# Second attention: scores four steps ahead of the transposes, and three smaller reorderings

## The reference

```python
# first block, mixer: cb, cc, ch are three projections of the normalized x
y_conv = cb * causal_dwconv3(cc * ch, conv_w)
y_conv = group_rms_norm(y_conv, conv_norm_g, CONV_GROUPS)
h = h + concatenate([y_conv, y_ret]) @ w_out
# second block, 8 heads of 64 of each kind, causal, 512 x 512
y_fox = softmax(q_f @ k_f.T / 8 + F[t] - F[s]) @ v_f          # F: cumulative log forget gate
sel   = top_k(sum_h w_i[t, h] * relu(q_i @ k_i.T / 8), 128)    # keys that each query may see
y_dsa = softmax(q_d @ k_d.T / 8 + bias, over sel) @ v_d
merged = sigmoid(gate_fox) * (y_fox @ w_branch_fox) + sigmoid(gate_dsa) * (y_dsa @ w_branch_dsa)
x = x + gate1 * (merged @ w_out)
```

## Time and profile before

| | us |
|---|---|
| median of three runs | 1446.51 |
| profiled execution | 1447.23 |
| its span | 1445.4 |
| PE busy | 1378.2 (95%) |
| DVE busy | 807.1 (56%) |
| POOL busy | 570.1 (39%) |
| ACT busy | 515.1 (36%) |

### The profile page before, as it was taken

The page is one execution under the profiler, slowest core; times in us unless marked ns, Lnnn a source line. Parts: engine busy times, 40 slices in busy tenths (PEclk is TensorE's granted clock), DMA queues, the critical chain, the costliest instruction groups (busy, mean ns, idle before and its releaser), DMA issues.

```text
span 1445.4 us, 18266 instructions
## 1 busy us (share of the span) xinstructions
PE 1378.2 (95%) x6154; PEld 1099.1 (76%) x6158; DVE 807.1 (56%) x1096; ACT 515.1 (36%) x771; POOL 570.1 (39%) x230
## 2 busy tenths in 40 slices
PE   7899999999999999999888889999989999999997
PEld 5677777888788888876665566788868888888886
DVE  6555567484765847868877676311235534253353
ACT  4333224332323323234345455423344323142243
POOL 3334334454462634424212122344433645445341
PEclk9999999999999999989999999999999999999998
DMA  7643234365574646522312222233332423324221
GB/s 199 130 88 91 70 102 132 104 180 153 153 204 142 187 129 179 135 73 74 88 44 72 60 74 73 73 102 102 94 95 73 130 74 115 88 86 117 73 88 58
DMA packets 238985, 155.46 MB, mean 108 GB/s; under 512 B 7860, under 2 KB 229424, under 8 KB 238808
## 3 DMA queue, kind: packets, MB, share of 16 engines
q1 hardware_dynamic: 238472, 153.56, 37.9%
q10 hardware_dynamic: 464, 1.27, 0.3%
HBM read 150.08 MB, written 4.73 MB: 107 GB/s over the span
## 4 chain that ended last, share of the span: by engine, by line
PE 42%; DVE 11%; issue 1%; ACT 0%; another core or an unknown queue 0%; DVEq 0%; ACTq 0%
PE ps L504 35%; PE ps L870 3%; DVE work L1744 2%; DVE top L1742 2%; PE ps L783 1%; PE ps L771 1%; DVE prob L1784 1%; DVE probt_even L1799 1%; DVE work L1762 1%; DVE prob L1792 1%; PE ps L757 1%; DVE xres L1695 0%; PE ps L758 0%; DVE q_dn L1811 0%; DVE work L1759 0%
## 5 line engine op out<-in xcount | busy, mean ns | idle before, releaser
L467 POOL TENSOR_TENSOR w_lo<-raw,w_hi 128x1024 fp32r<-128x1024 f32 x222 | 566.2, 2558 | 843.4 <-ACT w_hi L940 838.6
L504 PE MATMUL ps<-u_hi,w_hi 128*128 128x512 f32 x1016 | 411.2, 405 | 18.7 <-DVEq L1814 6.9
L504 PE MATMUL ps<-u_hi,w_lo 128*128 128x512 f32 x1016 | 399.8, 394 | 0.0
L504 PE MATMUL ps<-u_lo,w_hi 128*128 128x512 f32 x1016 | 399.7, 393 | 0.0
L940 ACT ACTIVATE w_hi<-raw 128x1024 fp32r<-128x1024 f32 x221 | 231.7, 1053 | 209.8 <-PE ps L504 106.0
L504 PEld LDWEIGHTS ps<-u_hi,w_hi 128*128 128x128 f32 x1016 | 193.7, 191 | 66.6 <-issue 16.1
L504 PE MATMUL ps<-y_hi,w_hi 128*128 128x512 f32 x576 | 225.9, 392 | 1.5 <-POOL w_lo L467 1.4
L504 PE MATMUL ps<-y_hi,w_lo 128*128 128x512 f32 x576 | 224.9, 390 | 0.0
L504 PEld LDWEIGHTS ps<-u_hi,w_lo 128*128 128x128 f32 x1016 | 193.2, 190 | 41.7
L504 PE MATMUL ps<-y_lo,w_hi 128*128 128x512 f32 x576 | 224.8, 390 | 0.0
L504 PEld LDWEIGHTS ps<-u_lo,w_hi 128*128 128x128 f32 x1016 | 193.7, 191 | 40.5 <-issue 2.2
(11 more groups left out here) (228 smaller groups left out, 1396.7 us busy)
## 6 DMA issues: line engine op xcount, KB each, us to landing
raw<-w_in SPq DMA_DIRECT2D x69, 512.0 KB, 3.8
raw<-w_mlp SPq DMA_DIRECT2D x64, 512.0 KB, 4.0
adaw<-w_ada SPq DMA_DIRECT2D x32, 768.0 KB, 4.6
raw<-w_up SPq DMA_DIRECT2D x32, 512.0 KB, 6.2
raw<-w_down SPq DMA_DIRECT2D x32, 512.0 KB, 6.7
raw<-w_out SPq DMA_DIRECT2D x16, 512.0 KB, 3.8
bias_rows<-fbrow SPq DMA_DIRECT2D x4, 640.0 KB
xtok<-x SPq DMA_DIRECT2D x4, 512.0 KB, 6.1
```

Of the source, the lines that this page charges most:

```text
L467: pool.tensor_tensor(w_lo[:, s, :], raw[:, s, :], w_hi[:, s, :], ALU.subtract).then_inc(lo_ready[s], 1)
L504: last = pe.matmul(ps[0:cols, bank, :], w[:, s, c], r[:, k, :], start=(k == ks[0] and w is w_hi and r is r_hi), stop=(k == ks[-1] and w is ...
```

## The change

PE now makes the scores of tile-step n + 4 right behind the transposes of n, across the pairs' borders, with one part of a projection (two chunks, 6 matmuls) behind each; `prob` has four buffers. The projections run further ahead, and in the last pairs the gate units of two merge chunks are made. The merge then makes `branch(m - 1)` behind the units of chunk m, with banks in turn. DVE's and ACT's orders follow, the rounds are spread 13, 2, 1, 1, 1, 1, 1 ahead of the pairs and five in each of pairs 0 to 3, the last even copy goes to ACT (`turned_last`), and two reciprocals become one. In the convolution the third unit is begun ahead of `conv_sum`, and in the first output projection the casts stand two steps earlier.

```diff
+LOOK = 4
...
+    bra_order = [(0, 0), (1, 0)]
+    for m in range(KC):
+        bra_order += [(0, m + 1), (1, m + 1), (2, m)] if m + 1 < KC else [(2, m)]
...
+        prob_evens = sb("prob_evens", [P, 2, KEYROW], where=odd)
...
+        gates = sb("gates", [P, 4, T], where=keys_done)
...
-        prob = sb("prob", [P, 2, T], where=two)
+        prob_odds = sb("prob_odds", [P, 2, T], where=two)
...
+        def prob(n):
+            return (prob_evens, prob_odds)[n // 2 % 2][:, n % 2, 0:(n // 2 + 1) * P]
...
-            with pe.Fori(1, NQ) as j:
+            for j, cut in ((1, 5), (2, 3), (3, 0)):
                 unit(st_conv, 0, j, u_hi, u_lo)
                 unit(st_conv, 1, j, u_hi, u_lo)
+                if cut:
+                    unit(st_conv, 2, j, u_hi, u_lo, part=(0, cut), closes=False)
                 conv_sum(j - 1)
-                unit(st_conv, 2, j, u_hi, u_lo)
+                unit(st_conv, 2, j, u_hi, u_lo, part=(cut, KC), opens=(cut == 0))
...
-                if n >= 2:
-                    pe.wait_ge(sem("att_logit"), 8 * p + n - 1)
+                wait(pe, sem("att_logit"), 8 * p + n - 1)
...
-            def att(pieces, p, dsa):
-
-                def piece():
-                    pieces.pop(0)()
-                piece()
-                s_step(p, 0, dsa)
-                s_step(p, 1, dsa)
-                if p > 0:
-                    pv(p - 1)
-                piece()
-                for a in range(3):
-                    t_step(p, 2 * a)
-                    s_step(p, 2 * a + 2, dsa)
-                    t_step(p, 2 * a + 1)
-                    s_step(p, 2 * a + 3, dsa)
-                    piece()
-                t_step(p, 6)
-                t_step(p, 7)
-                piece()
-
-            def thirds(st, g):
-                def one(s, k0, k1):
-                    return lambda: unit(st, s, g, u_hi, u_lo, part=(k0, k1), opens=(k0 == 0), closes=(k1 == KC))
-                return [one(s, k0, k1) for s in range(2) for k0, k1 in ((0, 3), (3, 6), (6, KC))]
+            def pairs(st, s, i):
+                def one(k0):
+                    return lambda: unit(st, s, i, u_hi, u_lo, part=(k0, k0 + 2), opens=(k0 == 0), closes=(k0 + 2 == KC))
+                return [one(k0) for k0 in range(0, KC, 2)]
...
-            for s in range(2):
-                unit(st_att, s, 0, u_hi, u_lo)
-            for g in range(1, 2 * NQ):
-                att(thirds(st_att, g), g - 1, g > NQ)
-
+            pieces = [f for g in range(2 * NQ) for s in range(2) for f in pairs(st_att, s, g)]
+            pieces += [f for m in range(2) for s in range(2) for f in pairs(st_bra, s, m)]
+            for _ in range(KC + LOOK - 2):
+                pieces.pop(0)()
+            for n in range(LOOK):
+                pieces.pop(0)()
+                s_step(0, n)
+            for p in range(2 * NQ):
+                for n in range(8):
+                    if n == 0 and p > 0:
+                        pv(p - 1)
+                    t_step(p, n)
+                    coming = 8 * p + n + LOOK
+                    if coming < 16 * NQ:
+                        s_step(coming // 8, coming % 8)
+                    pieces.pop(0)()
 
             def branch(m):
                 pe.wait_ge(lo_ready[2], st_bra.turn(2, m) + 1)
-                wait(pe, bank_free[2], st_bra.turn(2, m))
-                for b, k0 in ((2, 0), (SA, NQ)):
+                wait(pe, bank_free[2], st_bra.turn(2, m) - 1)
+                for b, k0 in ((2 + m % 2, 0), (SA + m % 2, NQ)):
                     for k in range(k0, k0 + NQ):
                         pe.wait_ge(sem("att_y"), k + 1)
                         c = slice(k * P, (k + 1) * P)
@@ -872,13 +880,16 @@
                                              stop=(k == k0 + NQ - 1 and w is w_lo))
                 last.then_inc(used[2], 1)
 
-            att(thirds(st_bra, 0), 2 * NQ - 1, True)
+            pieces.pop(0)()
             pv(2 * NQ - 1)
+            for f in pieces:
+                f()
             branch(0)
-            with pe.Fori(1, KC) as m:
+            for m in range(2, KC):
                 unit(st_bra, 0, m, u_hi, u_lo)
                 unit(st_bra, 1, m, u_hi, u_lo)
-                branch(m)
+                branch(m - 1)
+            branch(KC - 1)
...
                 ahead(st_conv, 1, j)
+                ahead(st_conv, 2, j)
                 conv_root(j - 1)
-                ahead(st_conv, 2, j)
...
-                    if i > 0 or s >= AHEAD:
-                        ahead(st_out, s, i)
+                    n = i * 4 + s + AHEAD
+                    if n < KC:
+                        ahead(st_out, n % 4, n // 4)
...
+            def exps(p, n):
+                act.wait_ge(sem("att_logit"), 8 * p + n + 1)
+                act.activation(prob(n), prob(n), ACT.Exp, bias=mneg[:, n:n + 1], scale=-1.0,
+                               accum_out=rowsum[:, n:n + 1]).then_inc(sem("att_exp"), 1)
+            def turned_last(p):
+                act.wait_ge(sem("att_t"), 8 * p + 7)
+                act.activation(turned(probt_even, NT - 1), ps[:, TURNS[0], :].rearrange("p (j t) -> p j t", t=P), ACT.Copy
+                               ).then_inc(sem("probt_ready0"), 1)
...
+            exps(0, 0)
+            q_hi(1, False)
+            exps(0, 1)
+            q_hi(1, True)
+            ahead(st_att, 0, 1)
+            exps(0, 2)
+            exps(0, 3)
+            def gate_copy(s):
+                act.wait_ge(used[s], st_bra.turn(s, 0) + 1)
+                act.activation(gates[:, s, :], ps[:, s, :], ACT.Copy).then_inc(bank_free[s], 1)
+            def gate_first(s):
+                act.wait_ge(bank_free[s], st_bra.turn(s, 0) + 1)
+                act.activation(gates[:, s, :], gates[:, s, :], ACT.Sigmoid).then_inc(sem("gate_ready"), 1)
+            def gate(s, m):
+                act.wait_ge(used[s], st_bra.turn(s, m) + 1)
+                wait(act, sem("merged"), m - 1)
+                act.activation(gates[:, 2 * (m % 2) + s, :], ps[:, s, :], ACT.Sigmoid).then_inc(sem("gate_ready"), 1)
+                act.wait_ge(sem("gate_ready"), 2 * m + s + 1)
+                act.sem_inc(bank_free[s], 1)
+            def m_round(m):
+                act.wait_ge(sem("merged"), m + 1)
+                act.activation(m_hi[:, m, :], nt[:, 2, :], ACT.Copy).then_inc(sem("m_hi"), 1)
+            def coming_exp(p, n):
+                if 8 * p + n + LOOK < 16 * NQ:
+                    exps(p + (n + LOOK) // 8, (n + LOOK) % 8)
+            for p in range(2 * NQ):
                 if p > 0:
                     y_evac(p - 1)
+                coming_exp(p, 0)
                 turned_odd(p, 0)
+                coming_exp(p, 1)
+                if p + 1 < 2 * NQ:
+                    k_hi(p + 1)
+                else:
+                    gate_copy(1)
+                coming_exp(p, 2)
                 turned_odd(p, 1)
+                coming_exp(p, 3)
+                if p + 1 < 2 * NQ:
+                    ahead(st_att, 1, p + 1)
+                else:
+                    cast(st_bra, 1, 1)
+                    cast(st_bra, 2, 0)
+                coming_exp(p, 4)
                 turned_odd(p, 2)
+                coming_exp(p, 5)
+                turned_last(p)
+                if p + 2 < 2 * NQ:
+                    q_hi(p + 2, False)
+                elif p + 2 == 2 * NQ:
+                    gate_copy(0)
+                coming_exp(p, 6)
+                if p + 2 < 2 * NQ:
+                    q_hi(p + 2, True)
                 turned_odd(p, 3)
+                coming_exp(p, 7)
+                if p + 2 < 2 * NQ:
+                    ahead(st_att, 0, p + 2)
+                else:
+                    cast(st_bra, 0, p + 3 - 2 * NQ)
+            y_evac(2 * NQ - 1)
+            gate_first(0)
+            gate_first(1)
+            gate(0, 1)
+            gate(1, 1)
+            cast(st_bra, 1, 2)
+            cast(st_bra, 2, 1)
             m_round(0)
+            for m in range(2, KC):
                 gate(0, m)
+                if m + 1 < KC:
+                    cast(st_bra, 0, m + 1)
+                else:
+                    cast(st_out2, 0, 0)
                 gate(1, m)
+                if m + 1 < KC:
+                    cast(st_bra, 1, m + 1)
+                cast(st_bra, 2, m)
+                if m + 1 == KC:
+                    cast(st_out2, 1, 0)
+                m_round(m - 1)
+            m_round(KC - 1)
...
-            plan = selection_plan((2, 2, 2, 2, 24) + (0, 1, 1, 2) * NQ)
+            plan = selection_plan((2, 2, 2, 2, 13, 2, 1, 1, 1, 1, 1) + (1,) * 5 * NQ)
...
-                if n >= 2:
-                    dve.wait_ge(sem("att_t"), 8 * p + n - 1)
-                else:
-                    wait(dve, sem("att_t"), 8 * p)
+                wait(dve, sem("att_t"), 8 * p + n + 1 - LOOK)
...
+            def weights(p, i):
+                dve.wait_ge(sem("att_exp"), 8 * p + 2 * i + 2)
```

(69 more changed lines are left out.)

100 lines of the change are left out of this document (17 added, 83 removed).

## The result

The changed kernel takes 1427.95 us (median of 4 runs, 1425.77 to 1430.08) against 1446.31 of the kernel before beside it (1445.31 to 1447.16, 4 runs): ratio 0.9873, 95% interval 0.9854 to 0.9893. That is faster by 18.4 us (1.3%); the forecast said 1415.5, and 1427 at most. Its profiled execution took 1429.47, so 17.8 us are to be followed in the traces where the sum had 31.6.

What follows compares the result with a forecast made beforehand. PE, busy 95% of the span, was taken as the bound. From 40.5 us of waits and slow clock, costs of 0.65, 2.5, 2.2, 0.8, 1.6 and 5.8 went off, 3.0 and 1.6 came on: 31.55 won, 1415.5 us, range 1407 to 1427.

Steps and rivals of the forecast that it cites:

- The sum of idle and slow time: Query projection to last branch: 40.5 us to win if PE never waited: 32.2 idle, 5.8 extra wait cost, 2.5 slow clock.
- the 0.17s: PE waits in the attention stretch: each costs 0.17 us beyond its idle time, 5.8 us for 34 waits.
- Four steps of lead: Attention pairs: short PE waits go if DVE keeps pace; first-half pairs 18.8 us of DVE against 19.5 of PE.
- rival (a): Pairs 0 to 3: POOL passes block DVE's weights multiplies; 12 us at most, 8 likely, giving 1423.5; chance 0.18.
- Slot-1 weights: Attention pairs: weights come late, 0.75 us in each of three pairs, 2.2 us, and 0.8 in all for second-half pairs.
- Start of the stretch: Second block's first projections and pair 0: 0.65 us left of the 6.9 wait, and 2.5 us for DVE being behind.
- the 6.9 us wait: Second pair's projection waits for q_lows(0) behind 24 selection rounds; with 13 rounds, 0.65 us of wait left, for POOL.
- DVE's lag: Start of the attention pairs: DVE is behind, PE waits at the third transposes and for k_lows(1); 2.5 us taken.
- End of the merge: Last branch waits for slot 2's weights: new cost 5.8 us, 3.8 of wait and 2.0 of slow clock.
- Convolution and output projection: Ahead of the attention: 3.0 us won at the convolution sum, 1.6 at the first output projection's POOL wait.
- The narrow-wide changes: Attention pairs: two more changes between wide and narrow matmuls per pair, about 0.1 us each, 1.6 in all.
- tail, start and lag: Costs at the last merge branch (5.8 us), the second pair's projection (0.65) and DVE's being behind at the start (2.5).

Runs made afterwards that it cites:

- f_rptslot0: Changed kernel with a selection round moved to tile-step 7, last odd copy before q_hi, branch(6) between chunk 7's units, slot-0 cast right behind that copy: 1407.56 us, ratio 0.9741.
- e_front: Kernel before with only the convolution and output-projection edits ahead of the attention: 1442.19 us, ratio 0.9976.
- k_pv: Changed kernel with ACT's last odd copy of a pair ahead of q_hi(p + 2, True): 1424.80 us, ratio 0.9864.
- e_round: Changed kernel with one selection round of each of the first four pairs moved from tile-step 3 to tile-step 7: 1418.95 us, ratio 0.9816.
- k_cast: Changed kernel with the slot-1 cast moved on ACT to directly behind k_hi: 1426.36 us, ratio 0.987.
- e_castpv: Changed kernel with the edits of k_cast and k_pv together, without that of k_tail: 1418.17 us, ratio 0.9810.
- k_tail: Changed kernel with branch(6) between the two units of chunk 7 and its weights' cast ahead of the second gate on ACT: 1421.85 us, ratio 0.9838.
- e_after: The changed kernel once more, nothing altered: 1427.81 us, ratio 0.9874.

## Why the prediction was wrong, step by step

- **The sum of idle and slow time (40.5)** holds as what could be won. In f_rptslot0 37.5 us of gain were measured in all, 3.5 of them ahead of the attention, so 34.0 in the stretch; ten waits with 4.7 us are left there, 6.4 with the 0.17s: 40.4 together.
- **"Four steps of lead: PE stays the bound by 0.7 us a pair."** This is the step that failed, and it failed in the placing, not in the work. The work was forecast rightly. Where nothing is held (f_rptslot0) DVE is busy 18.18 us a pair, and the forecast left its 18.14 as they were (18.8 with the gaps); PE has 19.72, forecast 19.5. In the changed kernel DVE was busy 20.49: the pass over slot 1 started 0.16 us ahead of the second 512-wide multiply, which took 2.59 us instead of 0.49, and PE waited 2.15 to 2.17 us. I had counted the multiply 0.1 us ahead of the pass and gave that margin, 0.1 us in a chain of some twenty instructions, four chances in five. This is rival (a), in three pairs instead of four.
- **The price of the hold.** Rival (a) had 8 to 12 us for it, from 2 us a pair and 1 for slot 0. In the trace: three waits of 2.15 to 2.17 with their 0.17s, 7.0, and three stretches at half clock, 1.7 each, 5.1. I had taken from the earlier trace rows that 1.76 idle costs no clock and from the earlier trace rows that 2.37 does, and hadn't asked on which side 2.15 would fall. That 1.76 is safe doesn't hold either: in e_front a wait of 1.79 has a stretch at half clock behind it.
- **A step missed altogether:** ACT's last odd copy stands behind two evacuations of 0.59, and `pv`, the first work of the next pair, needs it: 6.15 us in six waits, with the 0.17s 7.2. The forecast followed DVE's order and the casts, but not this copy. The 7.2 is the length of the waits, not what the copy costs: moved ahead it gave 1.3 us alone (k_pv) and 1.1 on top of e_round and the tail (32.7 - 26.6 - 5.0), since the scores then waited for `k_lows`, which stands behind the held 256-wide multiply of slot 0. That one cured too, 4.7 more came.
- **Why the edits did not add.** k_pv leaves the held multiply, and so the waits of 2.14 to 2.18 and the slow stretches behind them. k_cast takes the hold away but keeps DVE full up to the value products, where PE then waits 2.00 to 2.28, with three slow stretches. Together they leave no wait over 1.04 in pairs 1 to 3 and no slow stretch (e_castpv). The order of the losses is a chain, PE to DVE to ACT and back to PE, in which a later link shows when the one before it is cured.
- **Slot-1 weights (2.2, and 0.8 in the second half)** appeared once, 0.71 in pair 0 (0.9 with its 0.17). In pairs 1 to 3 the longer wait for the even copy hides them. Where that wait is gone (e_round) it is there, 0.46 to 0.49 a pair; the forecast said 0.75.
- **Start of the stretch**: the 6.9 us wait became 0.51 (forecast 0.65), DVE's lag 0.82 and 0.34 us (1.5 with the 0.17s; forecast 2.5).
- **End of the merge**: 3.63 idle and 3.4 us at half clock, 5.3 (forecast 3.8 + 2.0); k_tail wins 5.0.
- **Convolution and output projection**: 1.00 us idle where 1.1 was forecast, the clock up behind it, the POOL wait gone; PE stands 4.6 us earlier there, as forecast. 1.2 of it had been given back when the attention began (698.04 against 701.45, 3.4 us): one stretch at half clock more at some 600 us. The profile of e_after, the same kernel, doesn't have it and is 4.3 us ahead of the kernel before at that place, so it differs from run to run; what brings it is open.
- **The narrow-wide changes (1.6)** can't be seen: a pair without waits took 19.62, and 19.9 was forecast without them.

The account of the 13.8 us that are missing, by the waits: the hold 12.1, the value products 7.2, clock ahead of the attention 1.2, and 0.5 lost again behind the merge (the last branch ends 18.3 us earlier, the span 17.7); less what was forecast and did not come, 2.1 (slot 1), 1.6 (narrow-wide), 1.6 (tail, start and lag). That is 15.7; 1.9 too much stays unassigned. By the runs: curing the hold gave 8.2 (e_round), the copy 1.1 on top of it, slot 0's hold 4.7, together 14.0, each of them to about 2 us. So the two steps that failed, no multiply held and no late copy, are worth about what was missing. Between whole runs it stays open as well how far the slow stretches near 600 us vary: the four runs of the changed kernel span 4.3 us.

## What to carry to other kernels

Where a VectorE operation and a GpSimd pass are released by the same event, do not count on which is first: move other work, or the cast, so that one is clearly ahead, and price both orders, with the wait and with what the clock then does. When a lead takes away one engine's waits, follow every other engine's order up to the first instruction of the next round, evacuations too, and look for a full engine in the part of the round ahead of the wait, not in the mean of the round. An edit that cures one late link and gains nothing isn't refuted before the link behind it has been cured as well.

## What the runs showed of the hardware

- A pass of POOL (two tensors from memory, 128x1024) and a DVE multiply from memory to memory do not run at the same time. The multiply that starts 0.16 us inside a pass of 2.46 takes 2594 ns instead of 0.49 us; one that starts 1.04 inside a pass of 2.40 takes 1.50 us instead of 0.35. MAX8 and the replacing pass keep their length inside a pass. These two stand in the pass from 739.83 to 742.45 of the earlier trace rows, and MAX8 has the 688 ns of the earlier trace rows:

```profile
740.95 0.69 DVE L1742 MAX8 top<-work 128x8 f32<-128x512 f32 x1
...
741.75 0.68 DVE L1744 MATCH_REPLACE8 work<-top,work 128x512 f32<-128x512 f32 x1
```

  The Trainium skill, SBUF — State Buffer, section on the two sides of the memory, states the lock of rival (a): the two exclude each other for a whole instruction. The trace agrees in length. If a multiply is running when the pass starts, the pass loses little: 2.46 and 2.62 against 2.39.
- Clock behind short waits: 0.51 to 0.56 for 3.4 us behind idles of 2.15 and 2.17, and none behind those of 1.56 us and less in pairs 0 to 5 of the changed kernel. But e_front has such a stretch behind 1.79, and k_cast has an idle of 2.27 at 764.11 and keeps the full clock behind it,

```profile
764.10:767.50 3.40, 3.39 (x22) 2.11 (x23) 2.06 (x7) 1.95 (x4) 1.98 (x1) 1.00 0.00 0
```

so the length of the one idle doesn't decide it alone. What does was not tried.
